# Fourier transform over channels of a two-block network, folded in halves before the matmul

## The reference, cut to what matters

```python
FN_GROUPS, FN_GC = 4, 256

def _fourier(u):
    B, T, _ = u.shape
    z = u.astype(jnp.float32).reshape(B, T, FN_GROUPS, FN_GC)
    y = jnp.fft.fftn(z, axes=(1, 3), norm='ortho').real
    return y.reshape(B, T, FN_W).astype(u.dtype)

def _merge(ym, yd, yf, g_pre, w_br_ml, w_br_da, w_br_fn, w_out):
    gm, gd, gf = jnp.split(jax.nn.sigmoid(g_pre), N_BRANCH, axis=-1)
    y = gm * (ym @ w_br_ml) + gd * (yd @ w_br_da) + gf * (yf @ w_br_fn)
    return y @ w_out
```

## Time and profile before

| what | value |
|---|---|
| runs | 3144.64, 3144.72, 3149.99 us; median 3144.72 |
| span of the profiled execution | 3145.2 us |
| PE busy | 3064.3 us, 97% |
| DVE, ACT, POOL busy | 1589.7, 604.8, 511.4 us |
| transform over channels, `l0` | 1716.59 to 1730.69 us |
| transform over channels, `l1` | 2832.59 to 2840.01 us |

### The profile page before, as it was taken

One profiled execution on the slowest core, in us unless ns is written; L12 is line 12 of the kernel. 1 busy time (PEld: TensorE's weight loads), 2 busy tenths in 40 slices (PEclk: granted clock), 3 DMA queues, 4 the chain that ended last, 5 costly groups with the idle time before them and its releaser, 6 DMA issues.

```text
span 3145.2 us, 38172 instructions
## 1 busy us (share of the span) xinstructions
PE 3064.3 (97%) x15762; PEld 2306.2 (73%) x15762; DVE 1589.7 (51%) x2383; ACT 604.8 (19%) x1195; POOL 511.4 (16%) x210
## 2 busy tenths in 40 slices
PE   8999999999999999999999999999999999999998
PEld 4458778775447856887588888888878888678544
DVE  6744541436865156325952348777424512722574
ACT  2104212131112012112621112110021211411111
POOL 4320000003432101112021112221110001000332
PEclk9999999999999999999999999999999999999999
DMA  5544532325552210232012133443322233233453
GB/s 220 205 170 178 192 140 105 134 88 225 173 195 81 80 54 27 97 105 94 19 76 81 54 143 138 146 155 129 120 107 81 81 134 112 77 141 114 171 177 118
DMA packets 51069, 388.09 MB, mean 123 GB/s; under 512 B 8400, under 2 KB 22864, under 8 KB 29008
## 3 DMA queue, kind: packets, MB, share of 16 engines
q1 hardware_dynamic: 46256, 380.40, 33.3%
q10 hardware_dynamic: 4640, 5.24, 0.8%
HBM read 371.72 MB, written 1.05 MB: 119 GB/s over the span
## 4 chain that ended last, share of the span: by engine, by line
PE 92%; DVE 5%; ACT 2%; issue 1%; DMA 0%; DVEq 0%; SPq 0%; ACTq 0%
PE bank L993 91%; PE bank L996 1%; DVE factors L2975 0%; DVE factors L2877 0%; DVE weights L2962 0%; DVE small L3604 0%; DVE h_T L2758 0%; DVE masks L3716 0%; DMA params<-params_dram 0%; ACT arena L2580 0%; DVE arena L3648 0%; DVE weights L2965 0%; DVE arena L2992 0%; ACT h_T L2070 0%; DVE arena L3559 0%
## 5 line engine op out<-in xcount | busy, mean ns | idle before, releaser
L993 PE MATMUL bank<-h_T,weights 128*128 128x256 f32 (+1 forms) x3184 | 776.5, 397 | 15.8 <-ACT h_T L2070 4.0
L993 PEld LDWEIGHTS bank<-h_T,weights 128*128 128x128 f32 x3184 | 602.8, 191 | 154.3 <-issue 68.2
L2687 POOL TENSOR_TENSOR weights<-weights 128x1024 f32<-128x1024 f32 (+2 forms) x103 | 257.7, 2502 | 1375.3 <-DMA weights<-wide_slabs_dram 1277.9
L2696 POOL TENSOR_TENSOR factors<-weights 128x1024 f32<-128x1024 f32 (+2 forms) x103 | 255.8, 2483 | 1226.9 <-PE bank L993 1043.3
L993 PE MATMUL bank<-arena,weights 128*128 128x256 f32 x1784 | 396.1, 381 | 4.9 <-DVE arena L3381 2.5
L993 PEld LDWEIGHTS bank<-arena,weights 128*128 128x128 f32 x1784 | 338.8, 191 | 54.3 <-DVE arena L3381 2.7
L993 PE MATMUL bank<-weights,h_T 128*128 128x256 f32 (+2 forms) x1040 | 341.2, 476 | 3.4 <-DMA weights<-wide_slabs_dram 2.0
L993 PE MATMUL bank<-factors,weights 128*128 128x256 f32 x1432 | 323.8, 379 | 3.5 <-DVE arena L2992 1.9
L993 PE MATMUL bank<-weights,factors 128*128 128x256 f32 (+1 forms) x936 | 301.7, 467 | 1.9 <-DVE weights L2962 1.3
L993 PEld LDWEIGHTS bank<-factors,weights 128*128 128x128 f32 x1432 | 271.8, 190 | 41.5 <-DVE arena L2992 2.7
L993 PEld LDWEIGHTS bank<-weights,h_T 128*128 128x128 f32 x1040 | 199.5, 192 | 127.4 <-issue 101.7
(11 more groups left out here) (353 smaller groups left out, 2616.0 us busy)
## 6 DMA issues: line engine op xcount, KB each, us to landing
weights<-wide_slabs_dram SPq DMA_DIRECT2D x155, 2048.0 KB, 7.8
arena<-wide_slabs_dram SPq DMA_DIRECT2D x44, 512.0 KB, 4.1
weights<-down_slabs_dram SPq DMA_DIRECT2D x8, 1408.0 KB, 5.9
merged_T<-arena SPq DMA_DIRECT2D x240, 32.0 KB, 1.9
arena<-arena ACTq DMA_DIRECT2D x16, 256.0 KB, 10.0
weights<-wide_slabs_dram SPq DMA_DIRECT2D x3, 1024.0 KB, 5.1
masks<-second_consts_dram SPq DMA_DIRECT2D x1, 2176.0 KB, 13.0
masks<-second_consts_dram SPq DMA_DIRECT2D x2, 1024.0 KB, 5.3
```

Source lines behind the costliest of these rows:

```text
L993: return mm(out, lhsT, rhs, start=start, stop=stop, skip_group_check=True)
L2687: nc.gpsimd.tensor_tensor(b[2], b[2], b[3], ALU.add).then_inc(S["first_sums"], 1)
L2696: nc.gpsimd.tensor_tensor(e, b[2], b[0], ALU.subtract).then_inc(S["first_sums"], 1)
```

## The change

The input channels of each group are put in another order by the layout of the weights (`FN_IN`): the low tile holds channels 0 to 127, the high tile 128 and then 255, 254, ... 129. So channels c and 256-c lie on one partition. DVE forms from the two tiles three arrays per group: the sums of the cosine part (`even_sums`, in place), the same with the sign of the high tile's partition 0 turned (`odd_sums`; `FOLD_SIGN` is -1 there; needed because channel 128 counts with (-1)^k), and the differences of the sine part. PE then multiplies one 128-channel tile per group in place of two, and makes only the output channels 0 to 127, ordered as the even ones and then the odd ones (`FN_OUT`): the even ones from `even_sums` to partitions 0 to 63 of the bank, the odd ones from `odd_sums` to partitions 64 to 127, and the sine part on all 128. Output channels 129 to 255 are the same halves joined with the signs exchanged; output channel 128 of each group is made by a last matmul of 32 columns (one nonzero column) for each group, all four in bank 4 on partitions 0, 32, 64 and 96, copied out by ACT and put on partition 0 of each second tile by DVE.

```diff
@@ PE @@
-                t.wait("act_for_pe", 4)
-                for k in range(KT):
-                    grp, half = k // 2, k % 2
-                    if k >= 4:
-                        t.wait("fn_halves")
-                    for f, out in enumerate(fn_parts(bank[4 + k % 4], ns)):
-                        for kk in range(2):
-                            last = matmul(out, dft_c[:, f, kk, half * P:(half + 1) * P], zf[:, 2 * grp + kk, 0:ns, (0, EVEN)[f]:(EVEN, T)[f]],
-                                          start=kk == 0, stop=kk == 1)
-                    last.then_inc(S["pe_for_act"], 1)
+                for g in range(4):
+                    even, odd = fn_parts(bank[4 + g], ns)
+                    even_sums, odd_sums, differences = fn_folded(g, ns)
+                    t.wait("fn_tiles")
+                    t.wait("fn_sums")
+                    matmul(even[0:64], DFT_COS[:, 0:64], even_sums)
+                    matmul(even[64:128], DFT_COS[:, 64:128], odd_sums)
+                    matmul(odd, DFT_SIN, differences).then_inc(S["pe_for_act"], 1)
+                t.wait("fn_halves")
+                for g in range(4):
+                    out = bank[4][32 * g:32 * g + 32, 0:ns * EVEN].rearrange("p (s t) -> p s t", s=ns)
+                    last = matmul(out, DFT_EDGE, fn_folded(g, ns)[0])
+                last.then_inc(S["pe_for_act"], 1)
                 t.wait("fn_halves", 4)
@@ ACT @@
-                for k in range(KT):
+                for g in range(4):
                     t.wait("pe_for_act")
-                    if k >= 4:
-                        t.wait("fn_out")
-                    t.out(af(FN_HALVES(k)[:, 0:nq], bank[4 + k % 4][:, 0:nq], ACT.Copy), "fn_halves")
-                t.wait("fn_out", 4)
+                    t.out(af(FN_HALVES(g)[:, 0:nq], bank[4 + g][:, 0:nq], ACT.Copy), "fn_halves")
+                t.wait("pe_for_act")
+                edge = fn_parts(bank[4], nq // T)[0]
+                t.step(af(FN_EDGES[:, 0:nq // T, 0:EVEN], edge, ACT.Copy))
+                t.out(af(FN_EDGES[:, 0:nq // T, T - 1:P:-1], edge[:, :, 1:P], ACT.Copy), "fn_halves")
+                t.wait("fn_out")
@@ DVE @@
-                for k in range(KT):
-                    even, odd = fn_parts(FN_HALVES(k), nq // T)
-                    y = A[:, k * 2 * T:k * 2 * T + nq].rearrange("p (s t) -> p s t", t=T)
+                for g in range(4):
+                    even_sums, odd_sums, differences = fn_folded(g, ns)
+                    high = ZF[:, 2 * g + 1, 0:ns]
+                    t.wait("fn_tiles", 2)
+                    t.step(stt(odd_sums, high[:, :, 0:EVEN], FOLD_SIGN, even_sums, mul, add))
+                    t.step(tt(even_sums, even_sums, high[:, :, 0:EVEN], add))
+                    t.out(tt(differences, differences, high[:, :, EVEN:T], sub), "fn_sums")
+                for g in range(4):
+                    even, odd = fn_parts(FN_HALVES(g), ns)
+                    y, mirrored = fn_tile(2 * g), fn_tile(2 * g + 1)
                     t.wait("fn_halves")
                     t.step(copy(y[:, :, 0:EVEN:P], even[:, :, 0:EVEN:P]))
+                    t.step(copy(mirrored[:, :, 0:EVEN:P], even[:, :, 0:EVEN:P]))
                     t.step(tt(y[:, :, 1:P], even[:, :, 1:P], odd, add))
-                    t.out(tt(y[:, :, T - 1:P:-1], even[:, :, 1:P], odd, sub), "fn_out")
+                    t.step(tt(y[:, :, T - 1:P:-1], even[:, :, 1:P], odd, sub))
+                    t.step(tt(mirrored[:, :, 1:P], even[:, :, 1:P], odd, sub))
+                    t.step(tt(mirrored[:, :, T - 1:P:-1], even[:, :, 1:P], odd, add))
+                t.wait("fn_halves")
+                for g in range(4):
+                    ins = copy(fn_tile(2 * g + 1)[0:1], FN_EDGES[32 * g:32 * g + 1, 0:ns])
+                    if g < 3:
+                        t.step(ins)
+                t.out(ins, "fn_out")
                 say("dve_for_pe")
```

More of the change, by code:

```diff
@@ L289 @@
 C2_N = 4352
+FN_IN = [*range(P), P, *range(T - 1, P, -1)]
+FN_OUT = [*range(0, P, 2), *range(1, P, 2)]
+FN_OUT += [P, *(T - c for c in FN_OUT[1:])]
 WKV_WORDS = 2048
@@ L536, in program @@
             "squares_ready", "squares_summed", "sums_ready", "means_ready", "roots_ready", "rstd_ready", "rstd_psum", "h_ready",
-            "shift_done", "lora_ready", "fn_halves", "fn_out",
+            "shift_done", "lora_ready", "fn_tiles", "fn_sums", "fn_halves", "fn_out",
             "pe_for_act", "pe_for_dve", "act_for_pe", "act_for_dve", "dve_for_pe", "dve_for_act",
@@ L911, in fn_parts, with FN_HALVES, fn_folded @@
             return (buf[:, 0:even].rearrange("p (s t) -> p s t", s=ns), buf[:, even:odd].rearrange("p (s t) -> p s t", s=ns))
-        def FN_HALVES(k):
-            return A[:, 12288 + (k % 4) * 512:12288 + (k % 4) * 512 + 512]
+        def FN_HALVES(g):
+            return A[:, 12288 + g * 512:12288 + g * 512 + 512]
+        def fn_folded(g, ns):
+            low = ZF[:, 2 * g, 0:ns]
+            odd_sums = A[:, 14336 + g * 2 * EVEN:14336 + g * 2 * EVEN + ns * EVEN].rearrange("p (s t) -> p s t", s=ns)
+            return low[:, :, 0:EVEN], odd_sums, low[:, :, EVEN:T]
+        FN_EDGES = A[:, 15376:15888].rearrange("p (s t) -> p s t", s=2)
+        DFT_COS, DFT_SIN = C[:, C2["dft_c"]:C2["dft_c"] + P], C[:, C2["dft_c"] + P:C2["dft_c"] + 2 * P]
+        DFT_EDGE, FOLD_SIGN = C[:, C2["dft_c"] + 2 * P:C2["dft_c"] + 2 * P + 32], C[:, C2["dft_c"] + 288:C2["dft_c"] + 289]
         def G_SQ(la):
@@ L1902, in channels @@
                         if k >= 4:
-                            t.wait("act_for_pe")
+                            t.wait("fn_tiles")
                         for s in range(ns):
@@ L2607, in _ @@
                     t.wait("pe_for_act")
-                    t.out(af(ZF[:, k, 0:nq // T], bank[4 + k % 4][:, 0:nq].rearrange("p (s t) -> p s t", t=T), ACT.Copy), "act_for_pe")
-                for k in range(KT):
+                    t.out(af(ZF[:, k, 0:nq // T], bank[4 + k % 4][:, 0:nq].rearrange("p (s t) -> p s t", t=T), ACT.Copy), "fn_tiles")
+                for g in range(4):
                     t.wait("pe_for_act")
-                    if k >= 4:
-                        t.wait("fn_out")
-                    t.out(af(FN_HALVES(k)[:, 0:nq], bank[4 + k % 4][:, 0:nq], ACT.Copy), "fn_halves")
-                t.wait("fn_out", 4)
+                    t.out(af(FN_HALVES(g)[:, 0:nq], bank[4 + g][:, 0:nq], ACT.Copy), "fn_halves")
[4 more added lines that the diff above has]
+                t.wait("fn_out")
                 if la == 0:
@@ L3845, in constants @@
         c2[:, t0 + k * T + EVEN:t0 + (k + 1) * T] = sin[k * P:(k + 1) * P, 1:P]
-        c2[:, d0 + k * 256:d0 + (k + 1) * 256] = cos[k * P:(k + 1) * P]
-        c2[:, d0 + 512 + k * 256:d0 + 512 + (k + 1) * 256] = -sin[k * P:(k + 1) * P]
+    c2[:, d0:d0 + P] = cos[0:P][:, FN_OUT[0:P]]
+    c2[:, d0 + P:d0 + 2 * P] = -sin[0:P][:, FN_OUT[0:P]]
+    c2[:, d0 + 2 * P] = cos[0:P, P]
+    c2[:, d0 + 288] = np.where(idx == 0, -1.0, 1.0)
     nf = 16
@@ L3980, in layout @@
         modulation(la)
-        moving(w[:, o + 3 * D:o + 4 * D], 512, blocks("fn"))
+        moving(w[:, o + 3 * D:o + 4 * D].reshape(D, 4, T)[:, :, FN_IN].reshape(D, D), 512, blocks("fn"))
+        w_fn = g["w_br_fn_2"][la].reshape(4, T, D)[:, FN_OUT].reshape(D, D)
         for half in range(2):
@@ L3984, in layout @@
             modulation(la)
-            stationary(g["w_br_fn_2"][la][:, 512 * half:512 * (half + 1)], blocks(f"fn_proj{half}"))
+            stationary(w_fn[:, 512 * half:512 * (half + 1)], blocks(f"fn_proj{half}"))
             modulation(la)
```

3 lines of the change are left out of this document (added).

## The result

| | before | after |
|---|---|---|
| runs | 6, 3142.21 to 3150.13 us | 6, 3126.74 to 3133.64 us |
| median | 3145.90 us | 3129.53 us |
| span of the profiled execution | 3145.2 us | 3128.9 us |
| token transform's second half to `fn_gate0`, `l0` | 22.71 us | 13.85 us |
| token transform to `fn_gate0`, `l1` | 15.53 us | 11.38 us |

The ratio after to before is 0.995, with a 95% interval of 0.9941 to 0.996: about 16 us less. In twelve runs of after (six of them from a later comparison) the median is 3130.3. The two last rows of the table run from the first matmul that writes banks 4 to 7 of the last four tiles (`l0`) or of all eight (`l1`) to the first matmul of `fn_gate0`. They are the measure in all that follows, since they see no more than the stage. They account for 8.86 + 4.15 = 13.0 us.

What follows compares the result with a forecast made beforehand. PE, busy 97% of 3145.2 us, was taken to bound the kernel. Savings of 9.5 us in `l0` and 4.5 in `l1` made 14.0, giving 3131.2, or 3130.7 against the median; range 3126 to 3134, with rivals to 3138.

Steps and rivals of the forecast that it cites:

- the sum: Over both channel transforms: 9.5 us less in `l0` plus 4.5 in `l1`, 14.0 us off, giving 3130.7 us.
- The kernel's limit and the chain: PE is busy 97% of 3145.2 us; the chain of waits around both transforms up to `fn_gate0` sets the gain.
- Side by side or not: PE's narrow products run abreast: a group's pair counts two steps in place of four, the last 8 records two.
- The change of width: PE going from full-wide to narrow products and back costs 0.22 us per group, bounds zero and 0.30.
- ACT's start behind PE: ACT's copy begins 0.2 us after the modelled end of PE's last record.
- The early start: PE's channel products start without waiting for the last `ZF` copy: 0.7 us of the gain in `l0`.
- ACT at the end: Two edge copies are the last link before `fn_gate0`: 0.39 us each in `l0`, 0.28 each in `l1`.
- The fold's slack: DVE's last fold ends before PE reaches group 3, by 1.0 us in `l0` and 0.4 in `l1`.
- DVE's tail: DVE's 11 us of joins and one-partition copies delay S4 for P3 first; cover 3.2 to 4.2 us, so no cost.
- (b): DVE's strided, reversed half rows cost more, in folds or tail, and PE waits: 3133 to 3138, put at 3136; chance 0.12.
- (c): Clock falls after norm stretches take the gain back: two or three longer ones leave 3138.4 to 3141 us; chance 0.08.
- (d): Transforms get slower through array emptying and half clock; a whole unit at half clock in `l0` gives 3154.8 us; chance 0.04.

Runs made afterwards that it cites:

- experiments 1: Kernel after, each half-wide pair made two zero-padded full-wide products: stages 14.19 us in `l0` and 10.90 in `l1`, against 13.85 and 11.38.
- experiment 2: Also `one_switch`: kernel after, reordered to one stretch of narrow products, ACT's edge copies ahead of its fourth half tile: stages 12.78 and 10.78 us, against 13.85 and 11.38.
- experiment 4: Also `tail12`: kernel after, DVE's last joining instruction repeated twelve times before the one-partition copies: stages 13.86 and 11.38 us; P6 2.04 us late.
- fold_once: Kernel after with only the input folded, all 256 outputs made by full-wide products: stages 14.79 us in `l0` and 12.63 in `l1`, against 13.85 and 11.38.
- best: Also the combined kernel: after with narrow products in one stretch and no PE wait for ACT's last copies before `fn_gate0`: stages 11.36 and 9.86 us, median 3129.0.

## Why the prediction held, and where it was off

The predicted 3130.7 us stands 1.2 us from the median of 3129.53. The mechanism is mostly the one given, but that the number is so close is in part luck: the stages gave 1.0 us less than the sum, and the runs of after stood some 3 us lower than the stages explain.

- **The kernel's limit and the chain** were read right: all of the gain lies between the token transform and `fn_gate0`.
- **Side by side or not**: right. The pair takes two steps, and the earlier trace rows carried over to it.
- **The change of width**: too small. I took 0.22 us in and out, with 0.30 as the upper bound; a group of 1.21 us less four records of 0.22 leaves 0.33, and 0.79 less 0.464 leaves 0.33 again. With three groups between the first half tile and the last, that is 0.33 late in each layer. The rule of the Trainium skill (TensorEngine Tiling (Array Packing), Key Properties), that changing the tiling mode drains TensorE, is borne out by the pauses of 0.33 and 0.39 us in the weight loads and by experiments 1 and 2. My reading of its price from modelled ends of records in the earlier trace rows was 0.1 us short.
- **ACT's start behind PE**: I took 0.2 us from the modelled end of the last record to ACT's copy. The rows say about 0.1: in the earlier trace rows the channel products end at 1730.69 and the copy starts at 1730.76, and in after the first group's last record ends at 1715.53 and the copy starts at 1715.63. The 0.1 too much hid the switch of the fourth group, which was 0.1 too cheap as well.
- **The early start** was in the sum: PE began the channel products 7.07 us after the second half of the token transform had begun, as predicted (7.08). Done alone it was worth 1.01 us in `l0`, where the text named 0.7 for it: the next product also starts 0.16 ahead of the modelled end of the one before, which makes it 0.91, and the 64 records took 13.98 us in place of 14.08. The sum had the 0.16 in its start; only the share was named too small.
- **ACT at the end**: the edge copies cost what was predicted (0.39 and 0.38; 0.28 and 0.28). The fourth half tile in `l0` was another 0.28 late, by the effect that before hides.
- **The fold's slack**: 1.4 us in `l0` (predicted 1.0), and in `l1` 0.7 (predicted 0.4), since the fold there ends at 2821.28 and group 3 starts near 2822.0. The rows' prices of the strided reads held: 0.49, 0.43 and 0.42 us.
- **DVE's tail**: its length was right (10.9 us against 11, the one-partition copies 0.44 each), and that it costs nothing too. Whom it would hurt first was wrong: not P3 through S4 but P6 through ACT's wait for `fn_out`. I had listed what was queued behind DVE's copies, and not what was queued behind ACT's wait for them. The cover was 3.5 us and not the sum's 3.2 to 4.2 by S4; close by chance.
- **The sum**: 14.0 predicted, 13.0 measured in the two stages; the missing 1.0 is the width (0.33 in each layer) and the late copy (0.28). The medians differ by 16.4. The other 3.4 go with the granted clock (0.0012 between the means, at 2.9 us for 0.001), which the sum doesn't have; the prediction had said 1.7 to 3.4 us either way for this. With 13.0 us off 3144.72 it would have been 3131.7, a microsecond above the prediction and inside its range.
- **Rivals** (b), (c) and (d) did not come. The wait of (b) shows as soon as PE is made faster (experiment 2) or DVE slower (experiment 4, there by way of ACT). In `fold_once` it costs 1.4 us. For (c) the prediction counted the falls at 1880, 2300 and 2930; the trace of before has five more ahead of 700 us, where the change can't move them.

## What to carry to other kernels

Before packing narrow products side by side, count the changes of width: here one in and out costs 0.33 us at 258 and at 129 columns alike, so it pays only where it saves more than that, and products of one width should stand together. A symmetry that halves the matmul also halves the tiles that follow, and buffers that are then used once can be worth as much as the matmuls. When work is added ahead of a signal, list what is queued behind the waiting instruction on every engine that waits for it. Savings of a few microseconds in a kernel of 3 ms are best read from stage lengths in the trace, and whole runs compared at the same granted clock, as long as it isn't the change that moves the clock.

## What was not expected of the hardware

- **A short stand can double, but need not.** In `tail12` PE stood 1.87 us, and the granted clock then fell for 3.4 us: 16 records took 5.41 in place of 3.62 us. In `fold_once` it stood 1.99 us before `fn_gate0` in `l1`, and the clock fell for 3.4 us again: 64 records took 15.77 in place of 14.08 us. The stands of 1.3 us ahead of `fn_gate0` in after have no fall behind them. The length of the stand alone doesn't decide it. Near 400 us after and `best` have the same code and a stand of 2.0 us; a fall follows in `best`, where the next 32 records took 3.63 us, and none in after, where they took 1.96:

```profile
400.56 1.96 PE L1006 MATMUL bank<-arena 64*64 64x128 f32 x32 [2.02 <-DVE arena L3204]
```

- **DVE and POOL hold each other up.** DVE's four sums of 1024 columns (L2991, L3000 in the combined kernel) took 5.00 us in after, where they end before POOL begins much of its own. In `one_switch` PE is earlier, so POOL starts within them, and they took 7.03; in the combined kernel they took 9.06:

```profile
1730.55 9.06 DVE L3000 TENSOR_TENSOR arena<-arena 128x1024 f32<-128x1024 f32 x4
...
1732.06 3.18 POOL L2721 TENSOR_TENSOR factors<-weights 128x1024 f32<-128x1024 f32 x1 [39.21 <-PE bank L1006]
...
1735.21 3.32 POOL L2712 TENSOR_TENSOR weights<-weights 128x1024 f32<-128x1024 f32 x1
```

The sums one by one show how: in the combined kernel two take 1.22 us as in after, and the two that meet an instruction of POOL take 3.26 (from 1733.07) and 3.25 (from 1736.36); in `one_switch` one meets POOL and takes 3.26. Each of these ends 1.08 us after the POOL instruction that it met, and each of POOL's ends 2.2 us after the sum of DVE that it met, so they look as if they ran in turns, a whole instruction at a time. POOL's two took 2.66 and 2.35 us in after. PE had no idle time here (busy 40.00 of the 40 us from 1725 on), so it cost nothing, but an earlier PE makes DVE's sums slower just where they are wanted sooner. The Trainium skill (GPSIMD Engine Reference, Specifications) states that GpSimd's SBUF interfaces are shared with VectorE and contend with its instructions with two SBUF inputs; these sums are of that kind, and the runs agree.
- **An instruction that starts 0.28 us late**: ACT's fourth of the channel stage in `l0`, in all the kernels here, whatever it copies; its cause stays open.
